# The two branch projections by block products, with one weight sum made by a DMA, in a hybrid RG-LRU and convolution trunk

## The reference, cut to what matters

```
hn = rms_norm(h, norm_g)                    # h: 16 meta rows + 512 rows, width 2048
xa, sa, vb, gb, sb, ma, mb = split(hn @ w_in)     # seven groups of 2048 columns
ya = rg_lru(conv4(xa)) * silu(sa)           # branch A
pa = ya @ w_proj_a
yb = silu(layer_norm(conv31(vb * sigmoid(gb)))) * silu(sb)   # branch B
pb = yb @ w_proj_b
merged = sigmoid(ma) * pa + sigmoid(mb) * pb
out = rms_norm(h + merged @ w_out, final_g)       # meta rows dropped
```

## Time and profile before

| | us |
|---|---|
| median of 3 runs | 1823.39 (1823.28 to 1824.08) |
| the profiled execution | 1824.23 |
| its span | 1822.7 |
| PE busy | 1791.8 |
| PE weight load busy | 1646.7 |
| DVE busy | 1279.1 |
| ACT busy | 666.3 |
| POOL busy | 120.8 |

### The profile page before, as it was taken

One profiled execution on the slowest core, in us unless ns is written; L12 is line 12 of the kernel. 1 busy time (PEld: TensorE's weight loads), 2 busy tenths in 40 slices (PEclk: granted clock), 3 DMA queues, 4 the chain that ended last, 5 costly groups with the idle time before them and its releaser, 6 DMA issues.

```text
span 1822.7 us, 28896 instructions
## 1 busy us (share of the span) xinstructions
PE 1791.8 (98%) x11732; PEld 1646.7 (90%) x11732; DVE 1279.1 (70%) x1610; ACT 666.3 (37%) x838; POOL 120.8 (7%) x134
## 2 busy tenths in 40 slices
PE   7999999999999999999999989999999999999998
PEld 7899999999999999988999989999888888888886
DVE  7969797979798888888888767888633333333431
ACT  5542424242424242423444444545422222222322
POOL 5400000000000000000000000000000000000000
PEclk9999999999999999999999999999999999999999
DMA  5233333333323233244444424444644433336422
GB/s 186 74 110 94 110 95 107 104 98 104 109 92 109 93 107 101 89 145 162 153 161 150 149 96 152 155 156 144 208 168 153 136 116 116 124 108 219 144 88 93
DMA packets 177888, 231.31 MB, mean 127 GB/s; under 512 B 6416, under 2 KB 154000, under 8 KB 177168
## 3 DMA queue, kind: packets, MB, share of 16 engines
q1 hardware_dynamic: 164800, 180.87, 30.6%
q0 software_dynamic: 13008, 49.29, 8.0%
HBM read 204.97 MB, written 25.17 MB: 126 GB/s over the span
## 4 chain that ended last, share of the span: by engine, by line
PE 87%; issue 7%; DVE 4%; ACT 1%; DMA 1%; POOL 0%; SPq 0%; POOLq 0%; ACTq 0%; DVEq 0%
PE psum L532 60%; PE psum L566 15%; PE psum L719 7%; PE psum L733 2%; PE psum L623 1%; DVE x_lo L1197 1%; DVE w_lo L1090 1%; DVE region L1516 1%; DMA aux<-conv_b_spill 0%; DMA region<-in_x_channels 0%; DVE region L1166 0%; ACT w_hi L748 0%; DVE w_lo L1324 0%; POOL aux L440 0%; POOL conv_b_spill L436 0%
## 5 line engine op out<-in xcount | busy, mean ns | idle before, releaser
L532 PE MATMUL psum<-x_hi,w_hi 128*128 128x264 f32 (+1 forms) x2144 | 553.0, 316 | 8.5 <-ACT w_hi L748 3.8
L532 PE MATMUL psum<-x_lo,w_hi 128*128 128x264 f32 (+1 forms) x2144 | 552.0, 316 | 0.0
L532 PEld LDWEIGHTS psum<-x_hi,w_hi 128*128 128x128 f32 x2144 | 353.7, 189 | 36.1 <-issue 7.3
L532 PEld LDWEIGHTS psum<-x_lo,w_hi 128*128 128x128 f32 x2144 | 353.5, 188 | 25.9 <-issue 0.2
L532 PE MATMUL psum<-x_hi,w_lo 128*128 128x264 f32 (+1 forms) x2144 | 354.8, 315 | 2.0 <-DVE w_lo L1090 2.0
L532 PEld LDWEIGHTS psum<-x_hi,w_lo 128*128 128x128 f32 x2144 | 308.3, 188 | 28.3 <-DVE w_lo L1090 2.4
L1112 DVE SCALAR_TENSOR_TENSOR region<-region,conv_cols 128x512 f32<-128x512 f32 x480 | 326.7, 747 | 0.0
L748 ACT ACTIVATE w_hi<-raw 128x1024 fp32r<-128x1024 f32 x128 | 135.7, 1060 | 435.7 <-PE psum L532 399.4
L1315 DVE TENSOR_TENSOR w_lo<-raw,w_hi 128x1024 fp32r<-128x1024 f32 x76 | 93.1, 1224 | 211.4 <-ACT w_hi L893 211.4
L1090 DVE TENSOR_TENSOR w_lo<-raw,w_hi 128x1024 fp32r<-128x1024 f32 x128 | 161.1, 1259 | 58.8 <-ACT w_hi L748 58.6
L893 ACT ACTIVATE w_hi<-raw 128x1024 fp32r<-128x1024 f32 x76 | 80.6, 1061 | 301.3 <-PE psum L532 273.2
(11 more groups left out here) (209 smaller groups left out, 2779.0 us busy)
## 6 DMA issues: line engine op xcount, KB each, us to landing
raw<-in_w_in SPq DMA_DIRECT2D x140, 512.0 KB, 3.5
region<-in_w_in SPq DMA_DIRECT2D x42, 1024.0 KB, 5.1
raw<-in_w_proj_a SPq DMA_DIRECT2D x32, 512.0 KB, 3.3
raw<-in_w_proj_b SPq DMA_DIRECT2D x32, 512.0 KB, 3.3
raw<-in_w_out SPq DMA_DIRECT2D x32, 512.0 KB, 3.8
aux<-conv_b_spill POOLq DMA_DIRECT2D x24, 512.0 KB, 4.5
region<-in_x_channels SPq DMA_DIRECT2D x8, 512.0 KB, 7.8
gated_a_spill<-wide POOLq DMA_DIRECT2D x8, 512.0 KB, 3.2
```

The costliest lines, as they stand in the source:

```text
L532: last = pe.matmul(psum[:, bank, 0:width], weights[:, s, k, m * P:(m + 1) * P], operand[part][:, place(4 * group + k), t0:t0 + width], sta ...
```

## The change

pa and pb become 16 more units behind the 21, so there are 37 units and no plain chunks of pa and pb. The operands of these units are seven blocks of ya (and later of yb) of 1 MB each, four of them sums or differences, prepared when ya and yb are spilled: DVE makes the sums (`ya_t_sums` in the bodies, `yb_t_sums` in the units of sb), POOL writes them to HBM. At the first unit of pa and the first of pb (`SWITCH`, units 21 and 29) SP reads the seven blocks back, each as soon as the last unit has used its predecessor, and ACT and DVE cut them to hi and lo. In the bodies `t_sums` moves from chunk 0 to chunk 6, `t_hi_of` from 2 to 8, and one tap from chunk 12 to chunk 0.

Within all units: the sum S1 = A21 + A22 is made by POOL's accumulating DMA, which reads A22 from HBM a second time and adds it onto the loaded A21; the signs of the other sums change; the order of the products is S1, S2, A12, S3, A11 of the next unit, A22, S4; ACT seeds a PSUM bank with minus the A11 product, so `copy_e1` and DVE's `read_u2` and `read_c21` turn into copies by ACT. In the last `def unit` of the diff, DVE's, p is the position of the product among the seven of a unit and i counts the pair of sb, pa or pb whose values are gated; `u` is `v - 2` and the loop over v in which `add_a22` stands is POOL's. `ya_t_sums` is four DVE operations of 256 numbers. The mean of squares moves to unit 10, its root to unit 11, its reciprocal to unit 12. Centred values are written back to HBM instead of being centred twice. sigmoid(ma) * pa is written to HBM, sigmoid(mb) * pb is added onto it there by an accumulating DMA, and merged is read back for the last product.

```diff
+        MA, MB, SB, PA, PB = range(5)
+        A11, S1, S2, A12, S3, A22, S4 = range(7)
+        UNIT = (S1, S2, A12, S3, A11, A22, S4)
+        SWITCH = {PA * PAIRS - STD: 0, PB * PAIRS - STD: 1}
             if W0 <= n < W0 + 4:
-                return min(n, W0)
+                return W0 - (n == W0)
+            def load_operand(v, q):
+                ...
+                sp.wait_ge(multiplied, chunk(v - 1, q) + 1)
+                sp.dma_start(token_operand(q)[1].bitcast(F32), operand_spill[n][spilled_block(q)])\
+                    .then_inc(operand_loaded[q], 16)
             for v in range(1, NV):
+                switch = v - 1 in SWITCH
+                if switch:
+                    load_operand(v - 1, A11)
                 load_blocks(v, 0)
+                if switch:
+                    for q in (S1, S2, A12):
+                        load_operand(v - 1, q)
                 load_blocks(v, 1)
+                if switch:
+                    for q in (S3, A22, S4):
+                        load_operand(v - 1, q)
+            def add_a22(v):
+                pool.wait_ge(block_loaded[2 * (v % 2)], 16 * (v // 2 + 1))
+                pool.dma_start(blocks[:, 2 * (v % 2), :, P:], w_source(STD + v)[1][:, :, P:], accum_op=ALU.add)\
+                    .then_inc(s1_summed[v % 2], 16)
+            for v in range(1, NV + 1):
+                ...
+                if v + 1 < NV:
+                    add_a22(v + 1)
+                if 0 <= u < PAIRS:
+                    pool.wait_ge(summed, CT + 2 * u)
+                    load_ln(conv_spill, u)
+                    spill_centred(u)
+            def unit(v):
+                wait(pe, c12_ready, v - 1)
+                wait(pe, c22_ready, v - 1)
+                product(v, S1, bank_of(v, 2), False)
+                pe.wait_ge(seeded, v + 1)
+                product(v, S2, bank_of(v, 1), True)
+                product(v, A12, bank_of(v, 0), True)
+                pe.wait_ge(u2_ready, v + 1)
+                product(v, S3, bank_of(v, 1), True)
+                if v + 1 < NV:
+                    first_product(v + 1)
+                pe.wait_ge(u3_ready, v + 1)
+                product(v, A22, bank_of(v, 1), True)
+                pe.wait_ge(c22_ready, v + 1)
+                product(v, S4, bank_of(v, 2), True)
-            TAPS = [0, 3, 3, 3, 3, 1, 1, 3, 2, 3, 2, 3, 3, 1, 0, 0]
+            TAPS = [1, 3, 3, 3, 3, 1, 1, 3, 2, 3, 2, 3, 2, 1, 0, 0]
+            def unit(v):
+                ...
+                for p, q in enumerate(UNIT):
+                    if p == 0 and v:
+                        read_c22(v - 1)
+                    if p == 3 and v:
+                        read_c12(v - 1)
+                    if q != A11:
+                        cut_lo_of(v, q)
+                    elif not last:
+                        cut_lo_of(v + 1, A11)
+                    if v + 1 in SWITCH and p == 3:
+                        operand_lo_of(v + 1, A11)
+                    if v + 1 in SWITCH and p == 6:
+                        operand_lo_of(v + 1, S1)
+                    if v in SWITCH and p in (0, 1, 2, 4, 5):
+                        operand_lo_of(v, UNIT[p + 1])
+                    if p == 0:
+                        sum_s3(v)
+                    if p == 2:
+                        sum_s4(v)
+                    if p == 3 and 0 <= i < PAIRS:
+                        scale_ln(i)
+                    if p == 4:
+                        if i >= PAIRS:
+                            gate_p(STD + v - 1)
+                    if p == 5:
+                        ...
+                        if 0 <= i < PAIRS:
+                            gate_yb(i)
+                            yb_t_sums(i, False)
+                    if p == 6:
+                        if not last:
+                            sum_s2(v + 1)
+                        if 0 <= i < PAIRS:
+                            yb_t_sums(i, True)
```

More of the change, by code:

```diff
@@ new lines, in chunk, with w_source @@
+        def chunk(v, q):
+            if q == A11:
+                return W0 + 7 * v - 2 if v else W0
+            return W0 + 7 * v + 1 + (UNIT.index(q) - (v == NV - 1 and q in (A22, S4)))
+        def w_source(w):
+            kind, i = divmod(w, PAIRS)
+            if kind in (PA, PB):
+                view = (w_pa_v if kind == PA else w_pb_v).rearrange("p (k h) n -> p h k n", h=2)
+                return [view[:, h, :, 256 * i:256 * i + 256] for h in range(2)]
+            column = (COL_MA, COL_MB, COL_SB)[kind] + 256 * i
+            return [w_in_v[:, KH * h:KH * (h + 1), ds(column, 256)] for h in range(2)]
@@ L291, in winograd_operands, with operand_source, token_operand @@
-            return a11, a21, a12, a22, sums3[:, v % 2]
+            return one[:, :, 0:P], one[:, :, P:], two[:, :, 0:P], two[:, :, P:]
+        def operand_source(v, q):
+            a11, a21, a12, a22 = winograd_operands(v)
+            return {A11: a11, S2: a11, S1: a21, S3: sums3, A12: a12, A22: a22, S4: a12}[q]
+        T_N1, T_T3, T_T4, T_T2 = range(4)
+        B11, B21, B22, T_BLOCKS = range(4)
+        def token_operand(q):
+            if q in (A11, A12, S4):
+                k, t = (0 if q == A11 else KH), META + (HS if q == S4 else 0)
+                return [part[:, k:k + KH, t:t + HS] for part in (x_hi, x_lo)]
+            b = {S1: T_N1, S2: T_T2, S3: T_T3, A22: T_T4}[q]
+            return [part[:, b] for part in (t_hi, t_lo)]
@@ new lines, in spilled_block, with spills, y_place @@
+        def spilled_block(q):
+            return {A11: B11, A12: B21, S4: B22, S1: T_BLOCKS + T_N1, S2: T_BLOCKS + T_T2, S3: T_BLOCKS + T_T3,
+                    A22: T_BLOCKS + T_T4}[q]
+        SWITCH = {PA * PAIRS - STD: 0, PB * PAIRS - STD: 1}
+        SWITCH_ORDER = (A11, S1, S2, A12, S3, A22, S4)
+        def spills(w):
+            return sum(32 if n // PAIRS == SB else 16 for n in range(w % 2, w, 2))
+        def y_place(j):
+            return 4 * (T_N1, T_T2, T_T3, T_T4)[j // 4] + j % 4
@@ L508, in _ @@
                 pool.dma_start(tokens[:, t, :], x_v[t]).then_inc(x_reloaded[t], 16)
+            for n in range(2):
+                pool.wait_ge(o_spilled[n], spills(5 * PAIRS + n))
             pool.wait_ge(multiplied, O0 + 2 * TT + 1)
@@ new lines, in seed, with read_u2, read_u3 @@
+            def seed(v):
+                act.wait_ge(multiplied, chunk(v, A11) + 1)
+                if v < 2:
+                    act.wait_ge(vb_gated, CT)
+                act.activation(bank(v, 1), bank(v, 0), ACT.Copy, scale=-1.0).then_inc(seeded, 1)
+            def read_u2(v):
+                act.wait_ge(multiplied, chunk(v, S2) + 1)
+                wait(act, c12_ready, v)
+                act.activation(u2, bank(v, 1), ACT.Copy, scale=-1.0).then_inc(u2_ready, 1)
+            def read_u3(v):
+                act.wait_ge(multiplied, chunk(v, S3) + 1)
+                wait(act, c22_ready, v)
+                act.activation(u3, bank(v, 1), ACT.Copy).then_inc(u3_ready, 1)
```

707 lines of the change are left out of this document (317 added, 390 removed).

## The result

The changed kernel takes **1830.4 us** (median of 7 runs, 1829.8 to 1835.2) against 1823.4 for the kernel before (7 runs, 1822.9 to 1824.1): a ratio of 1.0044, with an interval of 1.0033 to 1.0056. It is 7 us slower. Forecast were 1797, with a range of 1782 to 1814. The profiled execution took 1830.9 us, its span 1829.3.

What follows compares the result with a forecast made beforehand. PE, busy 98% of the span, was taken to bound the kernel. From the profiled 1824.2 us, gains of 42.6 and costs of 16 gave 1797.6, or 1797 against the median; the 8-in-10 range was 1782 to 1814.

Steps and rivals of the forecast that it cites:

- Step 6: Two switches: operand cuts put DVE behind and reads land late, costing 10 us (3 to 25).
- Step 7: Into the last stage: PE waits until ACT and DVE cut pair 0's merged tiles, costing 1 us (0 to 4).
- 1: pa and pb: 16 pairs at 21.94 us become 16 units at 20.0, gaining 31.0 us.
- 2: Unit 9: moving mean, root and reciprocal to later units removes PE's stall, gaining 9.6 us.
- 3: Into unit 0: the first cut waits for one chunk less, S1 for no DVE sum, gaining 2.0 us.
- 4: Branch bodies: added DVE work makes `c_lo` late, 0.55 us in each of seven rounds, costing 4 us.
- 5: Plain chunks of ma: four ya sums before DVE's cut of chunk 2 make it late, costing 1 us.
- 8: Accumulating DMA: lands in time for S1, costing 0; DMA share stays below about 0.65 outside the switches.
- A: All added costs hidden but 2 to 4 us, as DVE catches up and DMA has room: 1784 us, chance 15%.
- Rival B: DMA bounds the new units, through the norm's loop in units 2 to 9 or the switches: 1810 us, chance 15%.
- C: Slower than before: a slow accumulating DMA makes S1 set the length of a unit; chance 6%.
- D: The new places move unit 9's stall instead of freeing it: 1807 us, chance 4%.

Runs made afterwards that it cites:

- e2: Changed kernel with each of the 14 operand reads at the switches bringing only an eighth of its block, cuts whole: 1804.8 us in one run.
- e1: Changed kernel with S1 made by DVE and POOL's accumulating A22 reads removed: 1826.5 us in one run.
- e10: e9 with S1 made by DVE and no accumulating DMA of A22: 1811.6 us, ratio 0.9941 against the kernel before.
- e8: Changed kernel with SP reading three operands before the blocks and the A11 operand cut one position later: 1818.8 us in one run.
- e5: Changed kernel with 248 fp32r filling matmuls of 128 columns put into PE's holes at the switches: 1830.7 us.
- e9: e8 with the moved tap back in chunk 12 and POOL's last-stage reloads of x three products later: 1808.7 us, ratio 0.9919 against the kernel before.
- e11: e9 with the cuts of the A11 and A22 operands moved to position 5: 1810.5 us, ratio 0.9925 against the kernel before.
- e4: Changed kernel with 190 fp32 filling matmuls of 256 columns on spare data where PE idles at the switches: 1867.8 us.
- e3: Changed kernel with ACT and DVE cutting only an eighth of each operand at the switches, reads whole: 1811.8 us in one run.
- e7: Changed kernel with only an eighth of each operand both read and cut at the switches: 1793.2 us in one run.
- e6: Kernel before with root and reciprocal one unit later and unit 0's first cut waiting for one chunk less: 1814.0 us, ratio 0.9948.

## Why the prediction was wrong, step by step

**Step 6, the switches, failed.** The prediction put it as "Together 7 + 3 = 10 us", with 25 as the upper end; it is 39.5, and 29.5 us of the 33.4 by which the forecast missed are here. Each half of it was too small:

- The lag of DVE and ACT was to cost 7.6 us. With an eighth of each read 18.4 us are left (e2), of which a part still comes from reads, since ACT waits 13.7 us for them there. The durations were right: the cuts of 2048 numbers take 2.29 us on DVE and 1.91 on ACT, where I estimated 2.2 and 1.9. What was wrong was to count DVE's work as if DVE always had some. In e2 DVE waits 3.78 us before 1269.11, behind a read for which ACT waits 3.61 us, and ACT waits 4.07 us (before 1298.01) and 3.94 us (before 1313.51) for DVE. My 4.1 and 3.3 us of allowance knew no such waits. How much of the miss each of them makes is not shown.
- The late reads were to add 2.4 us; giving them back yields 21.1 (from 39.5 to 18.4). I had them landing after 9.4 us at worst. They take 12.7 at the median and 15.6 at worst; in the first switch SP and POOL issue almost 7 MB of transfers between 1255 and 1269 us. I also thought of a late read as of a delay to one cut. It stops everything behind it on ACT, then DVE, then PE. And two of the reads, S3 of each switch, were late before they were issued, behind a block load in SP's queue that waits for DVE: the lag of DVE comes back as a late read, and that as more lag.
- The rate was the third error, the smallest. I set 390 GB/s wanted against the 348 of the earlier trace rows. The first switch gets 254 GB/s at a share of 0.86. But e1, which takes the accumulating DMAs away and gives DVE their sums, gains 1.8 us of excess, e10 nothing, and e8 gains 12 us with all bytes in place: the order counts before the rate.
- The prediction has no term for the lower clock: 12.9 us of the 39.5 are products slower than 2.85 us. Filling the holes did not win them back (e5), and whether full clock alone would is open.

**Step 7, into the last stage,** was right for what it named (0.97 us for 1). It missed the 6.3 us inside the stage: PE's hole of 3.32 us at 1676.10, with matmuls at the lower clock behind it (0.43 us from start to start instead of 0.23), so that the stage takes 189.3 us instead of 183.0. In e9, e10 and e11, in which the reloads of x no longer come beside the last of merged, it is gone (183.1 us each). But it is gone in e2 (183.2) and e4 too, which haven't this edit, and is there in e1, e3, e5, e7 and e8: that these reloads cause it is likely and not shown.

**The steps that held.** 1: units of 19.93 us, 118.6 ns per matmul in pa and pb as in sb; with 21.94 before this is 32.1 us for the 31.0 forecast. The rule of the Trainium skill that spoke against the change ("TensorE: Matmul & The Clock Gate", Back-to-back issue gap), by which halving the columns would have lost 62 us, does not hold for these matmuls, which come every 118.6 ns with 256 columns and every 228.5 with 512. These are 9 and 13 ns over the other formula of the Trainium skill in that section, where the prediction has 12 for both. 2: unit 9 gives back 10.0 us, of which unit 10 takes 0.9 again, for 9.6 (in e6 it gives back 9.1, and unit 10 takes 2.4). 3: about 2 us, seen best in e6; in the changed kernel it is hidden under steps 4 and 5. 4: 0.7 us in each of the seven bodies, 4.7 us for 4. 5: 0.8 for 1. 8: PE waits for S1 in no ordinary unit. My bound on DMA there was wrong all the same (0.69 to 0.81 for "below about 0.65"), at no visible price in these units.

**The sum, once more with the measured sizes:** 1797.6 + 29.5 (step 6) + 6.3 (step 7) - 1.1 (step 1) + 1.2 (steps 2 and 4) - 0.2 (step 5) = 1833.3. PE's first product also began at 10.39 us instead of 12.06, which no step named: 1831.6, against 1830.9 in the profiled execution. That start is no gain of the change, since it also differs between kernels that are the same up to there (11.49 us in e9, 11.58 in e6).

**The rivals.** A falls with the 39.5 us. Rival B named a part of the mechanism, late DMA in the switches, and stopped at 25 us for it, so its 1815 was the end of my range. Its other place, the norm's loop, shows no wait of PE. C is refuted by the ordinary units, in which PE waits for no S1; the outcome came on its side of zero by another way. D did not come in the changed kernel, but in e6 2.1 us of the stall moved. The chance of "slower" was 6% because I let only one unlikely mechanism end there. The table of stretches had the warning: DVE at 83% in the stage, with 32 us of cuts to come for DVE and 27 for ACT in two places.

## What to carry to other kernels

A stage change that hands seven large operands through the engines which keep the pipeline going is priced by what stands behind each of them in the in-order queues, not by the sum of the work against the idle time. Put such reads ahead of loads that wait for a slow engine in the same queue: here this order, with one cut moved behind, was worth 12 of 39 us. Moving more of the cuts behind the copies that PE is about to need gained nothing on top (e11). And try the small repairs of a change on the kernel before first: two of them were worth 9 us there, while the change around them lost 16.

## What the hardware showed that I had not expected

**The accumulating DMA is dear for the DMA engines.** Taking it away gained this kernel little (e1, e10). Part 3 of the page, queues of the changed kernel, then the same of e1, which has 37 accumulating reads fewer:

```profile
q1 hardware_dynamic: 169568, 191.36, 32.6%
q0 software_dynamic: 58144, 87.57, 20.6%
```

```profile
q0 software_dynamic: 19664, 68.17, 11.6%
```

38480 packets with 19.4 MB take (0.206 * 1829.3 - 0.116 * 1824.9) * 16 = 2640 us of engine time, 69 ns for each packet of 504 bytes. The plain packets of q1 take 56 ns for 1128 bytes on average (0.326 * 1829.3 * 16 / 169568). Byte for byte that is 2.7 times as much. No plain DMA here moves rows of 512 bytes, so how much of it comes from the short rows and how much from the adding is not shown. The Trainium skill, "DMA: Bandwidth & Descriptors", Specifications, puts the least transfer for line rate at 512 B; an accumulating one of 512 B is not at it here. In a stretch of the first switch with one in flight the engines are all busy at a low rate, in the changed kernel and then in e1 (a packet counts whole in the stretch in which it starts, so a share can pass 1):

```profile
1265.00:1272.00 7.00, 6.56 (x56) 6.37 (x54) 0.00 (x0) 0.00 (x0) 0.00 (x0) 1.00 1.21 266
```

```profile
1265.00:1272.00 7.00, 6.75 (x58) 6.55 (x56) 0.61 (x2) 1.09 (x1) 0.00 (x0) 1.00 1.00 338
```

POOL needs 1.6 to 2.05 us to issue one, against some 0.73 for a plain read of that size. The accumulating write to HBM lands in 5.7 to 7.7 us.

**Keeping the clock up by filling bought nothing.** The switches ran at 0.84 and 0.94 of full clock; held at 0.97 and 1.00 by filling matmuls (e5) they took as long within 1.2 us. The fills took PE's time in the same places, so this is no price of the clock itself.
